# Turning the expert operands on TensorE instead of VectorE in a one-core mixture-of-experts layer

## The reference, cut to what matters

```python
def moe(h, router_w, router_b, w1, b1, w2, b2):     # h: [512, 1024], 32 experts, top 4
    logits = h @ router_w + router_b
    top_v, top_i = lax.top_k(logits, TOP_K)
    top_w = jax.nn.softmax(top_v, axis=-1)
    ...
    z = h[tok] @ w1[e] + b1[e]                       # w1[e]: [1024, 2048]
    z_glu, z_lin = jnp.split(z, 2, axis=-1)
    z_glu = jnp.minimum(z_glu, SWIGLU_LIMIT)
    z_lin = jnp.clip(z_lin, -SWIGLU_LIMIT, SWIGLU_LIMIT)
    act = z_glu * jax.nn.sigmoid(SWIGLU_ALPHA * z_glu) * (z_lin + 1.0)
    y = act @ w2[e] + b2[e]                          # w2[e]: [1024, 1024]
```

## Time and profile before

| | |
|---|---|
| median of 3 runs | 1660.35 us (1658.75 to 1662.87) |
| the profiled execution's own time | 1658.75 us |
| its span in the trace | 1656.6 us |
| TensorE busy | 1504.4 us (91%) |
| VectorE busy | 731.5 us (44%) |
| ScalarE busy | 265.3 us (16%) |
| moved by DMA | 497.14 MB, mean 300 GB/s |
| mean granted TensorE clock | 0.949 of full speed |

### The profile page before, as it was taken

One profiled execution on the slowest core, in us unless ns is written; L12 is line 12 of the kernel. 1 busy time (PEld: TensorE's weight loads), 2 busy tenths in 40 slices (PEclk: granted clock), 3 DMA queues, 4 the chain that ended last, 5 costly groups with the idle time before them and its releaser, 6 DMA issues.

```text
span 1656.6 us, 40828 instructions
## 1 busy us (share of the span) xinstructions
PE 1504.4 (91%) x14616; PEld 752.4 (45%) x14616; DVE 731.5 (44%) x2458; ACT 265.3 (16%) x443; POOL 217.2 (13%) x265
## 2 busy tenths in 40 slices
PE   5999999999995997999799799989788979898897
PEld 3668888888653232434243234434232424333233
DVE  4404877666647432434244244434242424343344
ACT  4403555555322000000000000000000000000001
POOL 1000000000152111111011112111111111111110
PEclk9999999999997998999899899999898979999998
DMA  8684111112438998966979989999899989999788
GB/s 359 199 262 138 52 51 51 51 51 55 162 150 330 405 418 362 372 272 259 415 318 403 417 328 397 413 417 400 362 376 417 415 363 365 417 410 416 316 324 321
DMA packets 130870, 497.14 MB, mean 300 GB/s; under 512 B 15372, under 2 KB 48492, under 8 KB 94908
## 3 DMA queue, kind: packets, MB, share of 16 engines
q1 hardware_dynamic: 122588, 479.99, 73.4%
q0 software_dynamic: 8256, 16.81, 2.7%
HBM read 484.92 MB, written 17.58 MB: 303 GB/s over the span
## 4 chain that ended last, share of the span: by engine, by line
PE 60%; DMA 19%; SPq 13%; DVE 4%; issue 3%; ACT 1%; POOL 0%; DVEq 0%; POOLq 0%; ACTq 0%
PE ps L1760 21%; PE ps L1798 11%; DMA big_b<-in_moe_w 9%; DMA arena<-in_moe_w 8%; SPq L430 7%; PE ps L1458 6%; PE ps L1460 5%; PE ps L1459 5%; SPq L424 3%; PE ps L1636 2%; PE ps L1583 1%; PE ps L1570 1%; PE ps L1481 1%; DMA ring_t<-in_mod_c 1%; PE ps L1579 1%
## 5 line engine op out<-in xcount | busy, mean ns | idle before, releaser
L1760 PE MATMUL ps<-arena,rows 128*32 128x512 f32 x2728 | 329.6, 619 | 34.1 <-DMA arena<-in_moe_w 30.1
L1760 PE MATMUL ps<-big_b,rows 128*32 128x512 f32 x2688 | 319.7, 610 | 28.6 <-DMA big_b<-in_moe_w 28.5
L860 ACT ACTIVATE rows<-ps 128x256 f32<-128x256 f32 x84 | 32.4, 386 | 1054.8 <-PE ps L1784 1021.9
L1760 PEld LDWEIGHTS ps<-arena,rows 128*32 128x32 f32 x2728 | 86.9, 112 | 230.0 <-issue 155.2
L1798 PE MATMUL ps<-big_b,rows 128*32 128x256 f32 x2688 | 169.1, 401 | 20.3 <-DMA big_b<-in_moe_w 20.3
L1760 PEld LDWEIGHTS ps<-big_b,rows 128*32 128x32 f32 x2688 | 84.7, 111 | 221.9 <-issue 151.7
L1798 PE MATMUL ps<-arena,rows 128*32 128x256 f32 x2688 | 167.3, 399 | 16.4 <-DMA arena<-in_moe_w 16.4
L1376 DVE SCALAR_TENSOR_TENSOR y_sb<-ps,w_s,g_q 128x256 f32<-128x256 f32 x42 | 20.3, 484 | 251.7 <-PE ps L1798 251.7
L1376 DVE SCALAR_TENSOR_TENSOR rows<-ps,w_s,g_q 128x256 f32<-128x256 f32 x42 | 20.3, 484 | 239.8 <-PE ps L1798 239.8
L1798 PEld LDWEIGHTS ps<-big_b,rows 128*32 128x32 f32 x2688 | 83.7, 114 | 85.7 <-DMA big_b<-in_moe_w 29.6
L1798 PEld LDWEIGHTS ps<-arena,rows 128*32 128x32 f32 x2688 | 83.8, 114 | 79.7 <-DMA arena<-in_moe_w 24.9
(11 more groups left out here) (365 smaller groups left out, 1840.2 us busy)
## 6 DMA issues: line engine op xcount, KB each, us to landing
arena<-in_moe_w SPq DMA_DIRECT2D x192, 1024.0 KB, 16.4
big_b<-in_moe_w SPq DMA_DIRECT2D x192, 1024.0 KB, 14.9
ring_t<-in_hg_w_in SPq DMA_DIRECT2D x32, 512.0 KB, 4.0
ogT<-in_mod_w SPq DMA_DIRECT2D x16, 1024.0 KB, 5.1
arena<-yrows SPq DMA_DIRECT2D x8, 1024.0 KB, 11.9
x_sb<-in_x SPq DMA_DIRECT2D x2, 2048.0 KB, 7.9
arena<-in_hg_w_in SPq DMA_DIRECT2D x4, 1024.0 KB, 25.6
arena<-in_mod_c SPq DMA_DIRECT2D x4, 1024.0 KB, 22.3
```

What stands on the lines that cost most here:

```text
L1760: last = mm(bank[q * G:(q + 1) * G, :], XT[par][:, pos * G:(pos + 1) * G], w[:, :, q * NW:(q + 1) * NW], start=(pos == 0), stop=False)
```

## The change

Both vector transposes of a block move to TensorE. TensorE turns `xg` with two 128x128 transposes into `ps[0]` after its chunk 5, and ScalarE copies the result to `XT` in two parts (columns for chunks 0 to 4 as `xt_ahead`, those for 5 to 7 as `xt_rest`). TensorE turns `act_a` with two more into `ps[6]` after chunk 2 of the next block, and ScalarE copies them to `aT2`. `XT` now has one buffer, and the SwiGLU intermediate has one of its own (`lin`). A full 128x128 transpose gives whole runs of the contraction index, so the host's new layout of the expert weights falls away; the chunks are read in the order `K_OF`.

```diff
@@ -35,6 +35,7 @@
...
 AHEAD = 5
+K_OF = (0, 2, 4, 6, 1, 3, 5, 7)
 NW = D // QT
@@ -256,7 +257,7 @@
...
-        XT, sig, act_a, aT2 = [mv(0), mv(3)], mv(1), mv(2), mv(4)
+        XT, sig, lin, act_a, aT2 = (mv(n) for n in range(5))
         xg = [mv(5), mv(6)]
@@ -288,7 +289,7 @@
...
         e_v_ok e_w_ok msk_ok tab_ps row_ok tab_ok
-        frow_st pt_ok xi_ps idx_ok rows_ok go xt_ok z_ps sig_ok at_ok y_ok
+        frow_st pt_ok xi_ps idx_ok rows_ok go xt_ps xta_ok xtb_ok z_ps sig_ok act_ok at_ps at_ok y_ok
         w1_used w2_used sel_ok ld_br ring_free h_st mrow_st ld_mrow wdT_ok b2_ok sum_ps fin_sq fin_std fin_ok out_st""".split()
@@ -421,7 +422,7 @@
...
             def load_w1(par, e, pos):
-                sp.dma_start(w1_slot(par, pos), moe_w1[bass.ds(e * D + pos * P, P), :]
+                sp.dma_start(w1_slot(par, pos), moe_w1[bass.ds(e * D + K_OF[pos] * P, P), :]
                              ).then_inc(ld_w1[par][pos], 16)
@@ -638,7 +639,7 @@
...
                     pool.wait_ge(S["idx_ok"], i * 2 + (par + 3))
-                    pool.wait_ge(S["xt_ok"], i * 2 + (par + 1))
+                    pool.wait_ge(S["xt_ps"], i * 2 + (par + 1))
                     pool.sem_inc(S["go"], 1)
@@ -851,13 +852,29 @@
...
+            NA = AHEAD * G
+
+            def xt_ahead():
+                A(XT[:, 0:NA], ps[0][:, 0:NA], ACT.Copy).then_inc(S["xta_ok"], 1)
+
+            def xt_rest():
+                A(XT[:, NA:NW], ps[0][:, NA:NW], ACT.Copy).then_inc(S["xtb_ok"], 1)
+
             A(junk[:, :], eps_t[:, :], ACT.Sigmoid)
+            act.wait_ge(S["xt_ps"], 1)
+            xt_ahead()
+            xt_rest()
             act.wait_ge(S["tab_ok"], 1)
...
                 for par in range(2):
+                    act.wait_ge(S["xt_ps"], i * 2 + (par + 2))
+                    xt_ahead()
                     act.wait_ge(S["z_ps"], i * 2 + (par + 1))
                     A(sig, ps[2 + par][:, 0:NW], ACT.Sigmoid, scale=ALPHA).then_inc(S["sig_ok"], 1)
+                    xt_rest()
+                    act.wait_ge(S["at_ps"], i * 2 + (par + 1))
+                    A(aT2, ps[6][:, 0:NW], ACT.Copy).then_inc(S["at_ok"], 1)
@@ -1201,11 +1218,6 @@
...
-            def transpose_x(par, count):
-
-                dve.wait_ge(ld_xg[par], count)
-                V.transpose(XT[par], xg[par]).then_inc(S["xt_ok"], 1)
-
             col = lambda n: idx_f[:, n:n + 1]
@@ -1324,7 +1336,6 @@
...
                                         kf4[:, :, k:k + 1].broadcast_to([P, LT, E]), ALU.mult))
-            transpose_x(0, 16)
             me.wait()
@@ -1348,13 +1359,12 @@
...
             base2 = me.base + me.count
-            n_in = 2 * 9 + 1
+            n_in = 2 * 8 + 1
             me.wait()
...
                 for par in range(2):
-                    transpose_x(1 - par, i * 16 + (par * 16 + 16))
                     dve.wait_ge(y_st[par], i * 16 + 16)
@@ -1365,11 +1375,11 @@
...
                     dve.wait_ge(S["sig_ok"], i * 2 + (par + 1))
-                    me.link(V.tensor_scalar(act_a, ps[2 + par][:, NW:2 * NW], 1.0 + LIMIT, 1.0 - LIMIT,
+                    me.link(V.tensor_scalar(lin, ps[2 + par][:, NW:2 * NW], 1.0 + LIMIT, 1.0 - LIMIT,
                                             ALU.min, ALU.max))
-                    me.link(V.scalar_tensor_tensor(act_a, sig, SIG_MAX, act_a, ALU.min, ALU.mult))
-                    me.link(V.scalar_tensor_tensor(act_a, ps[2 + par][:, 0:NW], LIMIT, act_a, ALU.min, ALU.mult))
-                    V.transpose(aT2, act_a).then_inc(S["at_ok"], 1)
+                    me.link(V.scalar_tensor_tensor(lin, sig, SIG_MAX, lin, ALU.min, ALU.mult))
+                    V.scalar_tensor_tensor(act_a, ps[2 + par][:, 0:NW], LIMIT, lin, ALU.min,
+                                           ALU.mult).then_inc(S["act_ok"], 1)
                     choose(1 - par, i * 2 + (par + 1))
@@ -1752,17 +1762,25 @@
...
+            def transpose_x(par, count):
+
+                pe.wait_ge(ld_xg[par], count)
+                for s in range(2):
+                    last = tr(ps[0][:, s * P:(s + 1) * P], xg[par][:, s * P:(s + 1) * P], ident[:, :])
+                last.then_inc(S["xt_ps"], 1)
+
             def z_chunk(bank, par, pos, count):
...
                 for q in range(QT):
-                    last = mm(bank[q * G:(q + 1) * G, :], XT[par][:, pos * G:(pos + 1) * G], w[:, :, q * NW:(q + 1) * NW],
+                    last = mm(bank[q * G:(q + 1) * G, :], XT[:, pos * G:(pos + 1) * G], w[:, :, q * NW:(q + 1) * NW],
                               start=(pos == 0), stop=False)
...
             pe.sem_inc(S["w2_used"], W2C)
-            pe.wait_ge(S["xt_ok"], 1)
+            transpose_x(0, 16)
+            pe.wait_ge(S["xta_ok"], 1)
             for pos in range(AHEAD):
@@ -1777,16 +1795,24 @@
...
                     z, z_next, y = ps[2 + par], ps[3 - par], ps[4 + par]
+                    pe.wait_ge(S["xtb_ok"], i * 2 + (par + 1))
                     for pos in range(AHEAD, W1C):
                         z_chunk(z, par, pos, i * 16 + 16)
+                        if pos == AHEAD:
+                            transpose_x(1 - par, i * 16 + (par * 16 + 16))
                     pe.wait_ge(S["sel_ok"], i * 2 + (par + 1))
...
                     last.then_inc(S["z_ps"], 1)
-                    pe.wait_ge(S["xt_ok"], i * 2 + (par + 2))
+                    pe.wait_ge(S["xta_ok"], i * 2 + (par + 2))
                     for pos in range(AHEAD):
                         z_chunk(z_next, 1 - par, pos, i * 16 + (par * 16 + 16))
+                        if pos == 2:
+                            pe.wait_ge(S["act_ok"], i * 2 + (par + 1))
+                            for s in range(2):
+                                last = tr(ps[6][:, s * P:(s + 1) * P], act_a[:, s * P:(s + 1) * P], ident[:, :])
+                            last.then_inc(S["at_ps"], 1)
                     slots_of(i * 2 + (par + 4))
@@ -1795,7 +1821,7 @@
...
                             for q in range(QT):
-                                last = mm(y[q * G:(q + 1) * G, 0:NW], aT2[:, (2 * m + a) * G:(2 * m + a + 1) * G],
+                                last = mm(y[q * G:(q + 1) * G, 0:NW], aT2[:, a * P + m * G:a * P + (m + 1) * G],
                                           w2_slot(par, m, a)[:, q * NW:(q + 1) * NW], start=(m == 0 and a == 0),
@@ -1846,8 +1872,6 @@
...
     laid["mod_w"] = w[:, 2 * D:]
-    for name, n in (("moe_w1", 2 * FF), ("moe_w2", D)):
-        laid[name] = np.asarray(inputs[name]).reshape(E, QT, DK, G, n).transpose(0, 2, 1, 3, 4)
     for name in INPUTS:
```

## The result

| | kernel before | changed kernel |
|---|---|---|
| median of the runs, us | 1660.07 (1658.75 to 1662.87, 4 runs) | 1688.04 (1686.48 to 1690.22, 4 runs) |
| ratio, 95% interval | | 1.0167 (1.0149 to 1.0185) |
| profiled execution, us (span) | 1658.75 (1656.6) | 1680.55 (1678.8) |
| granted clock of TensorE, mean | 0.949 | 0.971 |
| the same in the loop, 538 to 1620 us | 0.94 | 0.97 |

The changed kernel is slower by 28 us in the runs, and by 22.2 us in the span of its profiled execution. That execution is faster than all four timed runs, so there are two things to explain: 22 us that the profile shows, and some 6 us that it does not.

What follows compares the result with a forecast made beforehand. Expert loop alternates between DMA and TensorE; only TensorE's time where DMA runs dry counts. 54 insertions x 0.39 = 21.1 us on 1658.75 gives 1679.8, and 1681.4 with the runs' median 1.6 higher; range 1667 to 1700.

Steps and rivals of the forecast that it cites:

- rival 1: Expert loop: insertions cost time in all 49 blocks where the chain runs over TensorE; 38.2 us, 1698.6 us; chance 0.10.
- rival 2: Expert loop: the inserted transposes do not overlap, each insertion costs 0.71 us; time 1698.7 us; chance 0.12.
- the forecast's 0.39: TensorE in the loop: us per inserted transpose pair, 0.23 for the pair plus 0.16 for returning to column groups.
- rival 3: Expert loop: the insertions are hidden anyway under DMA's 970 us; no more than 5 us, about 1662; chance 0.11.
- rival 4: Expert loop: faster, as VectorE's 0.45 us ahead of `ids` comes back in 27 blocks, 12 us; 1648; chance 0.05.
- The cross-check with `slots_of`: TensorE in the loop: four small matmuls in the same place cost 0.19 + 0.16 = 0.35 us, checking the 0.39.
- the 54 insertions: 31 x and 23 a transpose pairs in thirteen loop stretches where DMA runs dry; 21.1 us at 0.39 each.
- the granted clock in the loop changes: Sign of a wrong forecast: TensorE's granted clock in the expert loop changes; no size given.
- The stretch that ends at 1131.7: Loop stretch from 1101.6 us, TensorE setting the pace, counted with 3 x and 2 a insertions.
- the short stretches: Four loop stretches, before 666.2, 970.1, 1203.7 and 1571.17 us, counted with only one x insertion each.
- The wait for `act_ok`: TensorE after chunk 2 waits for the last SwiGLU step; 0.8 us said to be left.
- a new releaser in TensorE's stream: Sign of a wrong forecast: a new releaser stands ahead of L1760 or L1798 in the loop; no size given.

Runs made afterwards that it cites:

- The pairs alone: Kernel before plus two unread identity transposes on TensorE after chunk 5 and after chunk 2 of the next block; 1680.64 us against 1659.06, ratio 1.0137.
- the experiment that never leaves the column groups: Kernel before with the four whole-array slot-number matmuls split into sixteen in column groups; 1657.84 us against 1659.35, ratio 0.9983.

## Why the prediction was right, and where it was off

**What sets the price: as predicted.** It is TensorE's own time in the stretches where DMA has run dry. The pairs alone give +21.3 of the +22.2 us of loop part, while the layout and ScalarE's copies give nothing that can be seen. VectorE's lost work was never taken out alone, but the pairs leave no room for an effect of it. The lag grows from restart to restart by the counted insertions.

**The rivals.** The chain at its word (rival 1) foretold a pitch of 11.65 with 38 us lost. At the measured 1.01 us per block its 49 blocks would make 49.5 us; 22 were measured. Transposes that don't overlap (rival 2) foretold 0.71 per insertion; 0.505 was measured, between it and the forecast's 0.39, though the pair alone, 0.37, is well below 2 x 0.273. Hidden (rival 3) and faster (rival 4) fell with the first comparison. The version without any transposes bears on rival 4: VectorE's step ahead of `ids` is gone there and nothing is inserted, and still it is not faster than before.

**The term that was mis-sized.** "My value is 0.23 + 0.16 = 0.39 us per insertion": it measured 0.37 + 0.13 = 0.505. The return into column groups was near (0.13 for 0.16). The pair was not: 0.23 came from matmuls that use the whole array already, so it held no price for leaving the column groups. `slots_of` moved next to the x pair shows that part: the pair falls to 0.28 when another whole-array step stands ahead of it. The 0.05 us between that and 0.23 has no explanation here. The cross-check with `slots_of` (0.35) has a way in, but prices four tiny matmuls and not two transposes. At 0.505 the 54 insertions come to 27.3 us instead of 21.1.

The Trainium skill ("TensorEngine Tiling (Array Packing)", Key Properties) says that a change of tiling mode drains TensorE. That a change costs time, the traces bear out: 0.13 us behind each pair, and 0.22 us per block less in the experiment that never leaves the column groups. That it is a drain, no run here shows. The page gives no figure.

**What was missed, with a minus.** The forecast called itself wrong "if the granted clock in the loop changes", and it did, from 0.94 to 0.97 in the mean. Of the 27.3 us 22.2 came out. The stretch that ends at 1131.7 gave 2.2 us too few, 1.7 of it by a slow spell that stands in this profile of before; the short stretches gave some 2.5 too few. How much of this is the change's own is not shown. The slow spell is absent from two profiles with TensorE's work of before, and against these the changed kernel's loop part is 22.1 and 24.8 us longer. So the closeness to the predicted 21.1 is partly luck: two errors of opposite sign, +6 in the price and -5 (-2.5 to -5 by the profile that one compares with) in what reached the end.

**What was missed, with a plus.** The wait for `act_ok` was costed at nothing, with 0.8 us of slack, and a new releaser in TensorE's stream was named as a sign of being wrong. It came, ahead of the a pair. The profile of before shows 0.44 us from the bias to the sigmoid, and the slack was counted on it. The first profile of the changed kernel shows the same; in its second the time is over 0.7 us in 38 of 84 blocks (1.28 in the block shown), and then TensorE waits, with chunks 3 and 4, the slot numbers and `w2` behind. That is the likely source of the some 6 us between the profiled 22 and the timed 28. For it speak the timed runs of the pairs alone, whose excess (21.6 us in the median) is some 6 us under that of the changed kernel though the loop parts of the first profiles are alike, then the second profile (loop part +7.1, with the wait in its chain), and the version with the wait and no transposes: it should be free, costs 7.5 us, and TensorE waits 10.8 us on just that line. Only the profiled executions have a trace, so for the timed runs it stays likely and not shown. In the kernel before, the same chain of steps had to be done only at `w2`, behind two more chunks and the slot numbers.

**What stays open.** Why TensorE's signal comes late. The trace's record of the bias is no later, yet the semaphore's event is, and the sigmoid follows the event by 0.02 us; since the ends of matmuls are modelled, the records cannot say whether the bias itself ended late. It came in one of the two profiles of the changed kernel, in the one without transposes and in the one with the pair after chunk 4, and not in the profiles of the pairs alone, of `slots_of` moved or of the pair after chunk 3. Since one program shows it in one execution and not in another, the program alone does not explain it. Nor is it settled whether the 3.3 us gained by moving the pair to chunk 3 come from bearing it, nor why the mean clock of the loop rose.

## What to carry to other kernels

Price an inserted step in the form of its neighbours: a small whole-array matmul between column-group ones costs its own time, the way in and the way back (here 0.505 us for a pair that costs 0.23 among its like), so put such steps next to each other, or write them in the form of the stream. The shorter pitch did come here, but the time was not clearly better for it. Where DMA and the engine take turns as the limit, count the insertions only in the stretches where the queue has run dry; the chain names the engine in far more blocks than pay. A slack of less than a microsecond that one profile shows behind a wait on three engines in a row is no safe slack: place the wait one chunk later, if its result still has cover there, and take a second profile before costing the wait at nothing.

## What the hardware showed that was not expected

- A pair of float32 transposes of 128x128 costs TensorE's stream 0.23 us among whole-array matmuls, 0.28 behind the slot numbers and 0.37 among column-group matmuls, and 0.13 more goes into the chunks behind it.
- Sixteen tiny matmuls in column groups (0.10 us) are cheaper than four over the whole array (0.19) between the same neighbours, and `w2` behind them is 0.11 us shorter.
- The time from the start of the bias matmuls to the sigmoid that waits for them is 0.44 us in one execution and over 0.7 in 38 of 84 blocks of another of the same program. The late part is in TensorE's semaphore event; the sigmoid follows that by 0.02 us.
- A spell of slower clock behind a wait for weights (0.75 and 0.82 in two windows) was worth 1.7 us. It stood there in one profile of TensorE's work of before and not in two others, with 1.00 in the same place of the loop.
